# Attention inside a 920-unit weight stream: exponentials ahead of query rows, query rotation in three pieces, scores over 128 partitions

## What is computed

```python
def sliding_window_attention(h, positions, w_qkv, q_norm, k_norm, sinks, w_o):
    q, k, v = jnp.split(h @ w_qkv, ...)          # 32 query heads, 4 key/value heads, 64 wide
    q = apply_rope(rms_norm(q, q_norm), cos, sin)
    k = apply_rope(rms_norm(k, k_norm), cos, sin)
    ...                                          # two blocks of 128 queries, keys of own and previous block
    scores = jnp.where(valid, einsum(q, k) * 64 ** -0.5, -inf)
    m = jnp.maximum(jnp.max(scores, axis=-1), sink)
    p = jnp.exp(scores - m)
    probs = p / (jnp.sum(p, axis=-1) + jnp.exp(sink - m))
    return einsum(probs, v) @ w_o
```

## Time and profile before

| | |
|---|---|
| median of 3 runs | 2745.18 us (2743.76 to 2745.23) |
| profiled execution, its own time | 2745.03 us |
| its span, first to last instruction | 2743.7 us |
| TensorE busy | 2714.3 us, 99% |
| VectorE, ScalarE busy | 61%, 50% |
| mean granted TensorE clock | 0.997 |

### The profile page before, as it was taken

How to read it: one execution, slowest core, us unless ns; L and a number is a source line. 1 busy time by engine, 2 the same in 40 slices (tenths; PEclk the granted TensorE clock), 3 DMA queues, 4 the chain that set the end, 5 groups by cost and what they waited for, 6 DMA issues and landing times.

```text
span 2743.7 us, 34702 instructions
## 1 busy us (share of the span) xinstructions
PE 2714.3 (99%) x13940; PEld 2298.2 (84%) x13940; DVE 1685.0 (61%) x2438; ACT 1371.8 (50%) x2040; POOL 0.2 (0%) x4
## 2 busy tenths in 40 slices
PE   9999999999999999999999999999999999999998
PEld 7667888888888888888888888888888888888886
DVE  6676566556655664565555655544568756775675
ACT  6665544444434455445444644444455535553554
POOL 0000000000000000000000000000000000000000
PEclk9999999999999999999999999999999999999999
DMA  7334666666666667768696566554566566656654
GB/s 234 112 96 145 185 188 189 193 185 191 187 198 187 182 191 189 170 147 178 188 192 219 172 187 187 190 153 151 183 181 207 184 203 179 199 182 202 187 184 146
DMA packets 256995, 495.54 MB, mean 181 GB/s; under 512 B 17202, under 2 KB 18482, under 8 KB 256323
## 3 DMA queue, kind: packets, MB, share of 16 engines
q1 hardware_dynamic: 256834, 493.33, 61.4%
HBM read 491.17 MB, written 2.10 MB: 180 GB/s over the span
## 4 chain that ended last, share of the span: by engine, by line
PE 97%; ACT 2%; DVE 1%; DMA 0%; issue 0%; SPq 0%; ACTq 0%
PE ps L445 29%; PE ps L434 16%; PE ps L436 16%; PE ps L435 16%; PE ps L450 15%; PE ps L424 1%; PE ps L516 1%; PE ps L619 1%; PE ps L680 1%; PE ps L661 1%; PE ps L536 0%; ACT sS L950 0%; ACT whi L861 0%; DMA raw<-in_attn_w_qkv 0%; PE ps L585 0%; DVE wlo L1278 0%
## 5 line engine op out<-in xcount | busy, mean ns | idle before, releaser
L861 ACT CAST whi<-raw 128x1024 fp32r<-128x1024 f32 x920 | 967.1, 1052 | 1234.0 <-PE ps L436 633.7
L1278 DVE TENSOR_TENSOR wlo<-raw,whi 128x1024 fp32r<-128x1024 f32 x920 | 1121.8, 1222 | 675.8 <-ACT whi L861 674.8
L445 PE MATMUL ps<-XA,whi 128*128 128x512 f32 x1792 | 449.1, 392 | 0.0
L445 PE MATMUL ps<-XC,whi 128*128 128x512 f32 x1664 | 416.9, 392 | 0.0
L434 PE MATMUL ps<-whi,XB 128*128 128x512 f32 x960 | 377.1, 393 | 0.0
L436 PE MATMUL ps<-whi,XB 128*128 128x512 f32 x960 | 374.2, 390 | 0.0
L435 PE MATMUL ps<-wlo,XB 128*128 128x512 f32 x960 | 374.2, 390 | 0.0
L445 PEld LDWEIGHTS ps<-XA,whi 128*128 128x128 f32 x1792 | 322.6, 189 | 57.9
L445 PEld LDWEIGHTS ps<-XC,whi 128*128 128x128 f32 x1664 | 299.5, 189 | 53.7
L434 PE MATMUL ps<-whi,XA 128*128 128x512 f32 x736 | 293.2, 398 | 0.3 <-DVE wlo L1278 0.3
L436 PE MATMUL ps<-whi,XA 128*128 128x512 f32 x736 | 287.9, 391 | 0.0
(11 more groups left out here) (225 smaller groups left out, 1894.2 us busy)
## 6 DMA issues: line engine op xcount, KB each, us to landing
raw<-in_w_up SPq DMA_DIRECT2D x176, 512.0 KB, 3.8
raw<-in_w_in SPq DMA_DIRECT2D x128, 512.0 KB, 4.9
raw<-in_ffn_w_gate SPq DMA_DIRECT2D x88, 512.0 KB, 3.8
raw<-in_ffn_w_up SPq DMA_DIRECT2D x88, 512.0 KB, 3.8
raw<-in_ffn_w_down SPq DMA_DIRECT2D x88, 512.0 KB, 4.0
raw<-in_w_down SPq DMA_DIRECT2D x88, 512.0 KB, 3.7
raw<-in_w_ckv SPq DMA_DIRECT2D x64, 512.0 KB, 4.0
raw<-in_attn_w_qkv SPq DMA_DIRECT2D x40, 512.0 KB, 4.2
```

The lines of the kernel that those rows point to most:

```text
L445: pe.matmul(ps[:, b, :], whi[:, i, j, c], both, start=w.begin and j == 0, stop=False)
L861: act.copy(whi[:, u % NSPL, :, :], raw[:, u % NRAW, :, :]).then_inc(s.hi, 1)
L1278: dve.tensor_tensor(wlo[:, u % NSPL, :, :], raw[:, u % NRAW, :, :], whi[:, u % NSPL, :, :].bitcast(F), ALU.subtract).then_inc(s.lo, 1)
```

## The change

Five edits, all in the attention:

1. ScalarE does `exponents(n)` right behind `whi` of its step, ahead of `query_rows` and `query_root`; and its `queries` copies come behind `chances` and `values`.
2. VectorE's query rotation is split in three. `query_first` (Q+1) now ends with the products with `ropeB` for `t = 0` (`rotate_swap`), `query_second` (Q+2) finishes `t = 0` (`rotate_sum`), `query_third` (Q+3) rotates `t = 1`. For c = 0 all three run at Q+1.
3. The negated sinks and scales are kept (`minus`), so that `maxima` has three small instructions in place of four behind its reduction.
4. The scores contract over 128 partitions: `qT` holds two heads one above the other, `kT` is there twice, with the keys in the upper or the lower 64 partitions and zeros in the others (two memsets on VectorE at step 12, waited for by ScalarE's `keys`).
5. ScalarE therefore copies `qT` in 2 instructions of 128 partitions in place of 4 of 64, and `kT` in 8 of 64x256 in place of 8 of 64x128.

```diff
-    qT = [space["C"].take(f"qT{i}", [64, 8, 256]) for i in range(2)]
+    qT = [space["C"].take(f"qT{i}", [P, 4, 256]) for i in range(2)]
-    kT = M.take("kT", [64, 4, 256])
+    kT = [M.take(f"kT{i}", [P, 4, 256]) for i in range(2)]
...
-                e = pe.matmul(ps[:, b, m * nk:(m + 1) * nk], qT[c % 2][:, h, qb * P:(qb + 1) * P], kT[:, c, 0:nk],
-                              start=False, stop=m == len(heads) - 1)
+                e = pe.matmul(ps[:, b, m * nk:(m + 1) * nk], qT[c % 2][:, h // 2, qb * P:(qb + 1) * P],
+                              kT[h % 2][:, c, 0:nk], start=False, stop=m == len(heads) - 1)
...
         def keys():
+            act.wait_ge(s.kzero, 1)
             act.wait_ge(s.ktr, 1)
-            for t in range(2):
-                for i in range(4):
-                    e = act.copy(kT[:, i, t * P:(t + 1) * P],
+            for i in range(4):
+                for half in range(2):
+                    e = act.copy(kT[half][64 * half:64 * half + 64, i, :].rearrange("p (t k) -> p t k", k=P),
...
         def queries(c):
             for t in range(2):
                 act.wait_ge(s.qtr, 2 * c + t + 1)
-                for h in range(2):
-                    e = act.copy(qT[c % 2][:, h:8:2, t * P:(t + 1) * P],
+                e = act.copy(qT[c % 2][:, :, t * P:(t + 1) * P],
...
         for u in range(U_END + 1):
-            if u in q_turn:
-                queries(q_turn[u])
             if u in p_turn:
                 chances(p_turn[u])
             if u in p_values:
                 values(p_values[u])
+            if u in q_turn:
+                queries(q_turn[u])
...
             while done <= split_until(u):
                 high(done)
                 done += 1
+            if u in ATTEND:
+                exponents(ATTEND[u])
...
             if u in q_root_at:
                 query_root(q_root_at[u])
-            if u in ATTEND:
-                exponents(ATTEND[u])
...
+            for half in range(2):
+                e = dve.memset(kT[half][64 - 64 * half:128 - 64 * half, :, :], 0.0)
+            e.then_inc(s.kzero, 1)
+            own.mark(dve.tensor_scalar(minus[:, 0:32], rows[:, 128:160], -1.0, None, ALU.mult))
...
-            own.mark(dve.tensor_scalar(ms, ms, 0.125, None, ALU.mult))
-            own.mark(rotate(qraw[c % 2], qtmp, "q", 8, 0))
+            dve.tensor_scalar(ms, ms, 0.125, None, ALU.mult).then_inc(s.qrs, 1)
+            dve.wait_ge(s.qrs, c + 1)
+            own.mark(dve.tensor_scalar(minus[:, 32 + (c % 2) * 16:48 + (c % 2) * 16], ms, -1.0, None, ALU.mult))
+            rotate_swap(qraw[c % 2], qtmp, "q", 8, 0)
 
         def query_second(c):
-            rotate(qraw[c % 2], qtmp, "q", 8, 1).then_inc(s.qrope, 1)
+            own.mark(rotate_sum(qraw[c % 2], qtmp, "q", 8, 0))
+
+        def query_third(c):
+            rotate_swap(qraw[c % 2], qtmp, "q", 8, 1)
+            rotate_sum(qraw[c % 2], qtmp, "q", 8, 1).then_inc(s.qrope, 1)
...
-            own.mark(dve.tensor_tensor(mx, mx, sink, ALU.max))
-            own.wait()
-            own.mark(dve.tensor_tensor(es, sink, mx, ALU.subtract))
-            own.wait()
-            dve.tensor_scalar(mx, mx, -1.0, None, ALU.mult).then_inc(s.mx, 1)
+            own.mark(dve.tensor_tensor(mx, mx, sink, ALU.min))
+            own.wait()
+            dve.tensor_tensor(es, mx, sink, ALU.subtract).then_inc(s.mx, 1)
...
+        q_second, q_third = ({u + n * (c > 0) + 1: c for u, c in Q.items()} for n in (1, 2))
```

More of the change, by code:

```diff
@@ L198 @@
     act dve ones xtr xhi xlo sq rms rrt rs dg wd wide res
-    table sine rope mask kv ksq kms krt krope ktr kT
+    table sine rope mask kzero kv ksq kms krt krope ktr kT
     qe qsq qms qrt qrs qrope qtr qT sco mx exp pn ptr pT pv bxh bx
@@ L261, in build @@
     sm = M.take("sm", [P, 160])
+    minus = M.take("minus", [P, 64])
     identb = M.take("identb", [P, P], BF)
@@ L904, in keys @@
         def keys():
+            keyT = ps[:, 4, :].rearrange("p (t j k) -> p t j k", t=2, k=P)
+            act.wait_ge(s.kzero, 1)
             act.wait_ge(s.ktr, 1)
-            for t in range(2):
-                for i in range(4):
-                    e = act.copy(kT[:, i, t * P:(t + 1) * P],
-                                 ps[64 * (i % 2):64 * (i % 2) + 64, 4, t * 256 + (i // 2) * P:t * 256 + (i // 2) * P + P])
+            for i in range(4):
+                for half in range(2):
+                    e = act.copy(kT[half][64 * half:64 * half + 64, i, :].rearrange("p (t k) -> p t k", k=P),
+                                 keyT[64 * (i % 2):64 * (i % 2) + 64, :, i // 2, :])
             e.then_inc(s.kT, 1)
@@ L932, in queries @@
                 act.wait_ge(s.qtr, 2 * c + t + 1)
-                for h in range(2):
-                    e = act.copy(qT[c % 2][:, h:8:2, t * P:(t + 1) * P],
-                                 ps[64 * h:64 * h + 64, (2, 0)[c % 2] + t, :].rearrange("p (i n) -> p i n", n=P))
+                e = act.copy(qT[c % 2][:, :, t * P:(t + 1) * P],
+                             ps[:, (2, 0)[c % 2] + t, :].rearrange("p (i n) -> p i n", n=P))
             e.then_inc(s.qT, 1)
@@ L1377, in mask_tables, with rotate_swap @@
             e.then_inc(s.mask, 1)
-        def rotate(src, tmp, n, nh, t):
+        def rotate_swap(src, tmp, n, nh, t):
             v = src[:, t, :].rearrange("p (h e) -> p h e", e=64)
@@ L1385, in rotate, with rotate_sum @@
             own.mark(e)
+        def rotate_sum(src, tmp, n, nh, t):
+            v = src[:, t, :].rearrange("p (h e) -> p h e", e=64)
+            w = tmp[:, t, 0:nh * 64].rearrange("p (h e) -> p h e", e=64)
             own.wait()
@@ L1412, in key_rotate @@
             for t in range(2):
-                e = rotate(kraw, qtmp, "k", 4, t)
+                rotate_swap(kraw, qtmp, "k", 4, t)
+                e = rotate_sum(kraw, qtmp, "k", 4, t)
             e.then_inc(s.krope, 1)
@@ L1438, in attend @@
             nh, nk = len(heads), 128 * (qb + 1)
-            at, q = 40 + 12 * (n % 8), (c % 2) * 16 + qb * 8 + heads[0]
+            at, q = 40 + 12 * (n % 8), 32 + (c % 2) * 16 + qb * 8 + heads[0]
             mx, dn, es = (sm[:, at + 4 * j:at + 4 * j + nh] for j in range(3))
-            sink = rows[:, 128 + 8 * c + heads[0]:128 + 8 * c + heads[0] + nh]
-            return c, nh, nk, mx, dn, es, sm[:, q:q + nh], sink
+            sink = minus[:, 8 * c + heads[0]:8 * c + heads[0] + nh]
+            return c, nh, nk, mx, dn, es, minus[:, q:q + nh], sink
         def maxima(n):
@@ L1715, in vector @@
         inverse_at = later(ROOT, 1)
-        q_first, q_second, p_values = later(Q, 1), later(Q, 2), later(ATTEND, 3)
+        q_first, p_values = later(Q, 1), later(ATTEND, 3)
+        q_second, q_third = ({u + n * (c > 0) + 1: c for u, c in Q.items()} for n in (1, 2))
         tiles1, tiles2 = later(TILES, 1), later(TILES, 2)
@@ L1767, in vector @@
                 query_second(q_second[u])
+            if u in q_third:
+                query_third(q_third[u])
             if u in TILES:
```

## The result

| | before | changed |
|---|---|---|
| median | 2745.23 us | 2736.01 us |
| lowest to highest (7 runs each) | 2743.76 to 2746.76 | 2735.84 to 2739.01 |
| profiled execution, its own time | 2745.03 | 2737.57 |
| its span | 2743.7 | 2736.3 |

The ratio is 0.9968, with a 95% interval of 0.9959 to 0.9978: 9.2 us less, 0.34%. Forecast were 2743.5, and a range that ended at 2738. The forecast was wrong, and it gave "faster by over 0.2%" 17 in 100.

The account below looks back on a forecast made before the run. TensorE, busy 2714.3 of 2743.7 us, bounds the kernel; only attention waits and slow clock lie in reach. Chunks -2.9, clock +3.1, chunk 0 -0.7, shape -1.0 give -1.5 on 2745.03: 2743.5 us, range 2738 to 2747.

Parts of the forecast that it names:

- the price of the scores' shape: Attention scores on TensorE: leaving the 64-partition form was taken to save 1.0 us, between 0 and 2.9.
- the mask row: The mask's weight load, next to the scores: 0.26 us idle although no shape changes there; used to choose a low saving.
- the upper bound: Scores' shape: at most 0.19 us per group in 15 of 24 groups, 2.9 us in all.
- the rival with this rule: Scores' shape saves the whole 2.9 us, since changing the tiling mode drains TensorE: forecast 1.9 lower, 2741.6; chance 0.18.
- The clock: Behind the long waits of chunks 1 to 3: two slow stretches counted again, +3.1 us.
- a rival with 0.22: The clock stays up behind the new waits, or falls once: -1.5 to -3.1 us, 2740.4 to 2742; chance 0.22.
- The order: Reordered ScalarE and VectorE work in attention: -2.9 us over chunks 1 to 3 at full clock, -0.7 in chunk 0.
- The new wait at the query turn: Chunks 1 to 3: TensorE waits 2.8 us for the rotated queries before the query transposes.
- The values' wait: Chunk 1, second wait of TensorE for VectorE's values: 0.7 us instead of 2.55.
- my list: VectorE's work added up for steps 24 to 28 of chunk 1, from first division 92.6 to rotation end 110.5.
- the slower case: Exponentials' table load at step 26 comes behind the maxima's wait: 0.9 us later per chunk, +2.6, 2746.1; chance 0.12.
- The memsets and the later `keys`: Step 12: ScalarE's keys some 3 to 4 us later, hidden by the stream, costed at nothing; without cover 3 us once.

Follow-up runs that it names:

- s1: The changed kernel with the scores over 64 partitions again, the new orders on ScalarE and VectorE kept: median 2745.12 us, ratio to before 0.9999.
- s2: The kernel before with only the scores over 128 partitions and keys padded by zeros (and the memsets): median 2737.75 us, ratio 0.9971.
- s3: The changed kernel with ScalarE's exponentials behind the query rows and the root again: 2741.51 us, ratio 0.9983.
- s4: The changed kernel with the query rotation in two steps as before, first 128 tokens at Q+1, the others at Q+2: 2736.40 us, ratio 0.9966.
- s6: s5 with the whole query rotation moved to Q+2 (chunk 0's stays at step 17): 2725.94 us, ratio 0.9928.
- s7: s6 with the scores over 64 partitions again: 2731.81 us.
- t1: s1 with the mask laid head by head, so TensorE enters and leaves the 64-partition form more often: 2755.67 us, one time.
- t2: The changed kernel (scores over 128 partitions) with the mask laid head by head: 2740.91 us, one time.
- s5: s4 with VectorE's values ahead of wlo in each step, and at Q+2 the second rotation ahead of the division, wlo last: 2730.48 us, ratio 0.9944.

## Why the forecast was wrong

- **The step that failed is the price of the scores' shape.** "I take 1.0, nearer to the mask row." It measured 6.0, by s1 and s2 from both sides. Three things were wrong in it. The mask row's 0.26 is idle time that the changed kernel has too, so it said nothing on the shape and was no reason to leave the upper bound. The bound itself was too low, since it looked at the scores alone. Its 0.19 (1.05 less 0.86) came true to the digit, but it left out what the change of form does to the neighbours: 0.09 ahead of the first score and up to 0.11 behind the last one (1.71 is 0.32 + 1.05 + 0.34, and 1.32 is 0.23 + 0.86 + 0.23). Last, 18 groups count and not 15. 18 times 0.33 is 5.9.
- The Trainium skill, TensorEngine Tiling (Array Packing), Key Properties, says that changing the tiling mode drains the engine. The rows fit that, though none shows a drain as such: 0.23 and 0.33 us of idle loads at the two sides, gone with the change, and 64 switches cost 14.8 us where 24 cost 5.9. Weighed against it in the forecast was a row of another instruction type; the rival with this rule had 0.18 and, for want of the right bound, only 1.9 us.
- **The clock** was the other error. I counted two slow stretches, as in the trace of before. The profile has one, the median none: 3.1 us. That was a rival with 0.22, and its reason (2.54 without a slow stretch in the earlier trace rows) was the better reading: at a wait of this length one trace can't say. Which of the two it would be was luck: s1 has the same three waits at the query turn, and its times lie where two and three stretches would put them.
- With both put right the sum is 2743.5 - 5.0 - 3.1 = 2735.4, and measured are 2736.0. What is left is in the order's terms.
- **The order** was right. Forecast at equal clock: -2.9 + 3.1 in the chunks and -0.7 in chunk 0, in all -0.5; s1 says +0.2. The new wait at the query turn was forecast at 2.8 and is 2.54 to 2.57, three times. The values' wait was forecast at 0.7 and is 1.31 to 1.35, but 0.85 in s1, which has the order without the shape. TensorE gets there 10.5 us behind the first division (101.32 and 90.81) and by my list 11.0 (103.6 and 92.6): the shape of two groups saves there what this wait takes back. In chunk 0 the wait fell from 1.09 to 0.18, and the transposes then last 70.36 - 69.22 = 1.14 to the next start, for 0.85 before (from 69.88 to 70.73): 0.29 given back, as forecast.
- The table load, on which the slower case rested, wasn't late: VectorE waited 0.33 for group 5's exponentials, 0.4 by the forecast.
- The memsets and the later `keys` cost nothing that shows. ScalarE does wait 3.5 us for the memsets ahead of `keys`, as in the forecast, in s2 as in the changed kernel, but s2 is at 2736.05 all the same.
- The gain of the exponentials ahead is real, 2.3 us by s3, and so is the loss of the split in three, 4.2 by s4. The two don't add up singly, since each was measured beside the others; all of edits 1 to 3 together cancel within what s1 can tell.

## What to carry to other kernels

A bound read from a row must be about the same instruction: before a low value is taken for a suspected cost, ask whether the row would look the same without it. A high value read from the suspect alone isn't a bound either: measure from the instruction ahead of it to the second one behind. Here a matrix product over 64 partitions among others over 128 paid on both sides; padding it with zeros to 128 cost TensorE nothing that shows (s2), and it paid although the engine was 99% busy, since the gaps were counted as busy. Where one engine's list sets the waits, put the work that someone waits for ahead of the work with slack, and do the rest in one piece: s6 brought 10 us by this, and the split in three cost 4.

## What the runs showed of the hardware

- In and out of the 64-partition form between fp32 work over 128 partitions costs 0.33 us on the mean of 24 groups at 2.4 GHz, 0.39 with a product of 512 columns behind, 0.34 with transposes behind (s7 against s6), 0.24 to 0.29 with a bf16 mask on both sides (t1 against t2, one profile each).
- A slow stretch of TensorE costs 1.5 us and comes or stays away in the same program: behind waits of 2.5 to 2.6 us 2 of 3 fell before, 1 of 3 in the changed kernel, 0 of 3 in s2, 3 of 3 in s1. Behind waits of 2.55 to 2.7 in t1 and t2 it was 2 of 3 each, behind 2.8 (s4) 3 of 3, behind 2.25 (s3) and 1.8 (s5) 1 of 3 each, behind 0.9 (s6) none. Each of these is one profile. So a kernel with such waits has times in steps of 1.5 us, and a difference of 3 us between two of them can be clock alone.
- What sets the clock behind a 2.5 us wait stays open. s1 and s2 differ in it with nearly the same long waits, in their profiles and by their times; no run here took it apart.
